# One fused Trainium2 kernel of three transformer layers: how the second layer's output rows, the router's bias logits, the last norm's gain rows and the late expert loads are arranged

## What is computed

```
for i in range(2):
    x = x + 0.5 * swiglu(rmsnorm(x), ffn1)                    # D_FF = 2816
    q, k, v, q_m = split(rmsnorm(x) @ w_in[i])
    o_m = memory_attention(q_m, k_m, v_m)                     # 4 heads
    if i == 0: o_s = chunked_rel_attention(q, k, v, bias)     # 12 heads
    else:
        o = diff_attention(q, k, v, lam)                      # 6 heads of width 128
        o_s = rmsnorm(o, b_subln) * (1 - lambda_init)
    x = x + concat(o_s, o_m) @ w_out[i]
    x = x + 0.5 * swiglu(rmsnorm(x), ffn2)
t = moba_attention(x)                                         # 8 heads
h = layer_norm(alpha * x + t, ln_g[0], ln_b[0])
logits = h @ w_router + b_router                              # 32 experts, top 4
f = sum over the 4 chosen experts of gate * expert(h)         # 1024 -> 2048 -> 1024
out = layer_norm(alpha * h + f, ln_g[1], ln_b[1])
```

## Time and profile before

| | us |
|---|---|
| runs of the kernel | 2065.43, 2066.38, 2068.64 (median 2066.38) |
| the profiled execution, its time | 2069.82 |
| its span in the profile | 2068.0 |
| PE busy in the span | 1988.8 |
| DMA queue 1 | 602.79 MB, 74.9% of 16 engines |

### The profile page before, as it was taken

How to read it: one execution, slowest core, us unless ns; L and a number is a source line. 1 busy time by engine, 2 the same in 40 slices (tenths; PEclk the granted TensorE clock), 3 DMA queues, 4 the chain that set the end, 5 groups by cost and what they waited for, 6 DMA issues and landing times.

```text
span 2068.0 us, 29157 instructions
## 1 busy us (share of the span) xinstructions
PE 1988.8 (96%) x12306; PEld 1384.8 (67%) x12306; DVE 894.7 (43%) x1070; ACT 686.3 (33%) x941; POOL 39.1 (2%) x30
## 2 busy tenths in 40 slices
PE   8999999999999998999999999999999999999997
PEld 8998768999999886999998544444343333433343
DVE  6766666676666787666645211111111111111112
ACT  5545475545555566444444111111001000101011
POOL 0700000000000000000000000000000000000000
PEclk9999999999999998999999899999999999999999
DMA  9663607556556442555296999999999999999997
GB/s 317 196 223 131 235 1 257 191 184 200 170 190 208 166 162 74 173 202 184 95 333 247 372 426 427 427 428 428 429 428 429 428 429 428 429 428 429 428 429 318
DMA packets 165568, 603.88 MB, mean 292 GB/s; under 512 B 9324, under 2 KB 102464, under 8 KB 140564
## 3 DMA queue, kind: packets, MB, share of 16 engines
q1 hardware_dynamic: 165328, 602.79, 74.9%
q10 hardware_dynamic: 164, 0.04, 0.0%
HBM read 601.71 MB, written 1.09 MB: 291 GB/s over the span
## 4 chain that ended last, share of the span: by engine, by line
PE 69%; DMA 22%; DVE 4%; ACT 3%; issue 1%; SPq 0%; DVEq 0%; ACTq 0%
PE ps L1832 13%; PE ps L1834 13%; PE ps L1833 13%; PE ps L2412 12%; DMA sb_w_free<-in_moe_w_gate_up 7%; PE ps L2436 5%; DMA sb_raw<-in_moe_w_down 5%; DMA sb_raw<-in_moe_w_gate_up 3%; DMA sb_w_free<-in_moe_w_down 3%; PE ps L2382 2%; DMA sb_nat_more<-in_moe_w_gate_up 2%; DMA sb_late_raw<-in_moe_w_down 2%; ACT sb_w_hi L669 1%; PE ps L2444 1%; PE ps L2393 1%; DVE sb_w_lo L1112 1%
## 5 line engine op out<-in xcount | busy, mean ns | idle before, releaser
L1112 DVE TENSOR_TENSOR sb_w_lo<-sb_raw,sb_w_hi 128x2048 fp32r<-128x2048 f32 x175 | 403.0, 2312 | 233.8 <-ACT sb_w_hi L669 233.3
L669 ACT ACTIVATE sb_w_hi<-sb_raw 128x2048 fp32r<-128x2048 f32 x179 | 340.5, 1912 | 167.9 <-PE ps L1834 147.6
L1832 PE MATMUL ps<-sb_xT_hi,sb_w_hi 128*128 128x256 f32 x1344 | 373.2, 278 | 0.0
L1833 PE MATMUL ps<-sb_xT_lo,sb_w_hi 128*128 128x256 f32 x1344 | 372.7, 277 | 0.0
L1834 PE MATMUL ps<-sb_xT_hi,sb_w_lo 128*128 128x256 f32 x1344 | 372.6, 277 | 0.0
L1833 PEld LDWEIGHTS ps<-sb_xT_lo,sb_w_hi 128*128 128x128 f32 x1344 | 252.8, 188 | 1.5
L1832 PEld LDWEIGHTS ps<-sb_xT_hi,sb_w_hi 128*128 128x128 f32 x1344 | 252.3, 188 | 1.7 <-DVE sb_w_lo L1112 0.2
L1834 PEld LDWEIGHTS ps<-sb_xT_hi,sb_w_lo 128*128 128x128 f32 x1344 | 253.2, 188 | 0.0
L1027 ACT ACTIVATE sb_h_rows<-ps 128x512 f32<-128x512 f32 x32 | 19.2, 599 | 424.1 <-PE ps L2412 424.1
L1707 DVE COPY sb_h_rows<-ps 128x512 f32<-128x512 f32 x31 | 21.4, 692 | 317.2 <-PE ps L2412 317.2
L1834 PE MATMUL ps<-sb_w_hi,sb_a_lo 128*128 128x512 f32 x352 | 138.5, 393 | 0.0
(11 more groups left out here) (320 smaller groups left out, 2678.8 us busy)
## 6 DMA issues: line engine op xcount, KB each, us to landing
sb_raw<-in_moe_w_gate_up SPq DMA_DIRECT2D x49, 2048.0 KB, 34.5
sb_w_free<-in_moe_w_gate_up SPq DMA_DIRECT2D x46, 2048.0 KB, 34.5
sb_w_free<-in_moe_w_down SPq DMA_DIRECT2D x24, 2048.0 KB, 33.9
sb_raw<-in_ffn_w_up SPq DMA_DIRECT2D x44, 1024.0 KB, 5.3
sb_raw<-in_ffn_w_down SPq DMA_DIRECT2D x44, 1024.0 KB, 5.0
sb_raw<-in_moe_w_down SPq DMA_DIRECT2D x22, 2048.0 KB, 33.9
sb_raw<-in_ffn_w_gate SPq DMA_DIRECT2D x43, 1024.0 KB, 5.4
sb_late_raw<-in_moe_w_gate_up SPq DMA_DIRECT2D x17, 2048.0 KB, 35.2
```

Source lines behind the costliest of these rows:

```text
L669: sc.activation(w_hi[:, c % CUT, :], raw[:, c % RAW, :], ACT.Copy).then_inc(hi_made, 1)
L1112: ve.tensor_tensor(w_lo[:, c % CUT, :], raw[:, c % RAW, :], w_hi[:, c % CUT, :].bitcast(F32), ALU.subtract).then_inc(lo_made, 1)
L1832: pe.matmul(o, l_hi, r_hi, start=start, stop=False)
L1833: pe.matmul(o, l_hi, r_lo, start=False, stop=False)
```

## The change

1. **Second layer's output rows.** ACT and DVE cut the turned rows by block (`turn_block`, pieces of 2x128 columns), block 1 as soon as it is normed. `project_blocks` does the first column half of `w_out` for block 1, turns block 0 ahead of the last two of block 1's eight tiles, then does block 0. The second column half is as before. `sub_norm` is parted into `sub_mean` and the rest; block 1's mean and root come earlier.
2. **Bias logits.** The 8 matmuls of the bias logits, the router's weights and its bias row move from the router into the end of the second layer's attention, with three matmuls that nobody reads. Around the router there are fewer of those, and block 1's first `residual` comes behind the first expert's chunks.
3. **Last norm's rows.** Three pairs of single rows (4 KB each) are loaded early. POOL splits them into three 16-bit parts, and two sets of four matmuls (`spread_last_rows`) spread the gain and the bias over the partitions: the gain goes through PSUM to SBUF by ACT, the bias stays in PSUM. The two loads of 512 KB go.
4. **Late chunks.** The last gate and up chunk and both down chunks of expert 30 come in two DMAs each with a wait for each. The scatter of expert 30 stands between the halves of expert 31's first down chunk. The kept expert is 28 in place of 29, and the loop covers steps 4 to 27. The table for the root is loaded inside `last_two`.

```diff
-KEPT_E = N_E - 3
-LOOP_S = range(5, 9)
+KEPT_E = N_E - 4
+LOOP_S = range(4, 8)
...
+                else:
+                    sp.wait_ge(trig_gains, 4)
+                    sp.dma_start(wr[:], a["moe_w_router_2"][0].rearrange("(k p) e -> p k e", p=P)).then_inc(rel_loaded, 16)
+                    sp.dma_start(lg_row[:], rows(a["moe_b_router_2"][0], N_E)).then_inc(rel_loaded, 16)
...
+                sp.dma_start(dst[:, 0:1, :], src[:, 0:1, :]).then_inc(last_gate_row, 16)
+                sp.dma_start(dst[:, 1:2, :], src[:, 1:2, :]).then_inc(slot_loaded[(t + 3) % RING], 16)
...
+                src, dst = rows_of(N_E - 2, 0), slots[(t + 4) % RING].rearrange("p (a n) -> p a n", a=4)
+                sp.dma_start(dst[:, 0:2, :], src[:, 0:2, :]).then_inc(down_rows_0, 16)
+                sp.dma_start(dst[:, 2:4, :], src[:, 2:4, :]).then_inc(slot_loaded[(t + 4) % RING], 16)
...
+            for q in (32, 64, 96):
+                sp.dma_start(narrow_rows[q:q + 1, :], a["ln_g_2"][0, 1:2]).then_inc(ln1_loaded, 16)
+                sp.dma_start(narrow_rows[q + 1:q + 2, :], a["ln_b_2"][0, 1:2]).then_inc(ln1_loaded, 16)
...
-            sp.wait_ge(chunk_used, ROUND_C * more + (MOE_C0 + KEPT_T[1] + 1))
-            sp.dma_start(ln1_gain, rows(a["ln_g_2"][0, 1], D)).then_inc(ln1_loaded, 16)
-            sp.dma_start(ln1_bias, rows(a["ln_b_2"][0, 1], D)).then_inc(ln1_loaded, 16)
...
+            step(pool.memset(ln1_parts[:], 0.0))
+            for r in range(3):
+                src, part = (t[32 * r + 32:32 * r + 34, :] for t in (narrow_rows, ln1_parts))
+                for _ in range(r):
+                    step(pool.tensor_copy(part, src))
+                    step(pool.tensor_tensor(src, src, part, ALU.subtract))
+                step(pool.tensor_copy(part, src))
...
+                sc.wait_ge(ln1_spread, 2 * r + 1)
+                sc.activation(ln1_gain, ps[:, 2:4, :].rearrange("p a b -> p (a b)"), ACT.Copy).then_inc(gain_copied, 1)
...
+            def project_blocks(g, c0, t):
+
+                pe.wait_ge(proj_read, g - 1)
+                for b in (1, 0):
+                    for kk in range(KT):
+                        c, k = c0 + kk // 4, kk % 4
+                        if (b, kk) == (1, 6):
+                            turn(nat, [(sub_normed, 2)], (0,), last=0)
+                        if k == 0:
+                            pe.wait_ge(lo_made, c + 1)
+                        turned_tile(t + 1 - b, kk)
...
+                        if kind == "diff" and n == len(groups) - 2:
+                            pe.wait_ge(prob_made, u0 + n + 1)
+                            pe.wait_ge(rel_loaded, 64)
+                            keep_busy(1, 1)
+                            router_bias(range(4))
+                        elif kind == "diff" and n == len(groups) - 1:
+                            keep_busy(1, 1)
+                            router_bias(range(4, 6))
                         values(n)
+                        if kind == "diff" and n == len(groups) - 1:
+                            keep_busy(1, 1)
+                            router_bias(range(6, 8))
...
-                    keep_busy_from_biases(3, 2)
+                    keep_busy_from_biases(1, 2)
...
+            def spread_last_rows(row, bank):
+
+                for h in range(2):
+                    for half in halves:
+                        ins = pe.matmul(ps[half, bank + h, :], ln1_sel[:, row, :], ln1_parts[:, 512 * h:512 * (h + 1)],
+                                        start=True, stop=True)
+                return ins
...
+                down_rows(t + 6, 0, laps, r, own=last_own, bank=0, first_half=ahead_rows, between=scatter_here)
                 down_rows(t + 7, 1, laps, r, True, last_own, 0)
+                spread_last_rows(1, 1).then_inc(ln1_spread, 1)
                 scatter(last=e + 2)
```

More of the change, by code:

```diff
@@ L584, in _ @@
                     step_loads(4 * it + s, s, 3 * it)
-            step_loads(N_E - 3, N_E - 3)
+            for e in range(N_E - 4, N_E - 2):
+                step_loads(e, e)
             last_loads()
@@ L796, in tile_copies, with turn_block @@
                     ins.then_inc(tiles_copied, 1)
+            def turn_block(t, b, part):
+                for q in part:
+                    sc.wait_ge(turned, 4 * t + q + 1)
+                    src = ps[:, q, :].rearrange("p (k b t) -> p k b t", k=2, b=TB)[:, :, b]
+                    sc.activation(xT_hi[:, 2 * q:2 * q + 2, b * P:(b + 1) * P], src, ACT.Copy).then_inc(turn_hi, 1)
             def sub_root(b):
@@ L1081, in first_round @@
                         step(4 * it, s, 3 * it)
-                step(0, N_E - 3, 0)
+                for s in range(N_E - 4, N_E - 2):
+                    step(0, s, 0)
                 last_two(0)
@@ L1395, in remainder @@
                     for n in range(len(groups) + 1):
+                        if n == 7 and groups[-1]["diff"]:
+                            sub_mean(1)
                         if 1 < n < len(groups):
@@ L1803, in first_round @@
                         step(4 * it, 4 * it, s, 3 * it, 0)
-                step(0, 0, N_E - 3, 0, 0)
+                for s in range(N_E - 4, N_E - 2):
+                    step(0, 0, s, 0, 0)
                 last_two(0)
@@ L2205, in remainder, with router_bias @@
                         first_block()
+                def router_bias(ks):
+                    for k in ks:
+                        ins = pe.matmul(ps[:, 0, 0:N_E], gcol[:, 70 + k:71 + k].to_broadcast([P, P]), wr[:, k, :], start=k == 0,
+                                        stop=k == KT - 1)
+                    if ks[-1] == KT - 1:
+                        ins.then_inc(bias_logits, 1)
                 def moba_ahead():
@@ L2427, in down_rows @@
                 for k in range(4):
-                    if in_halves and k == 2:
+                    if between and k == 2:
+                        between()
+                    if first_half is not None and k == 2:
                         pe.wait_ge(slot_loaded[t % RING], loaded_no(t, laps, r))
```

153 lines of the change are left out of this document (101 added, 52 removed).

## The result

The changed kernel took 2054.49 us (median of four runs, 2053.82 to 2055.03) beside 2065.90 of the kernel before (four runs, 2064.81 to 2068.64): a ratio of 0.9939, 95% interval 0.9925 to 0.9953, or 11.4 us less. The forecast was 2055.1.

The account below looks back on a forecast made before the run. The weight stream was taken to run unpaused from the first free ring slot, which bounds the end. Gains of 5.0 + 3.9 + 2.4 = 11.3 us take the median from 2066.4 to 2055.1, range 2051.0 to 2061.0.

Parts of the forecast that it names:

- Term 1: Second layer's output rows: scaling and product start earlier by block; gain 5.0 us, range 3.4 to 7.1.
- Term 2: Router: bias logits, unread matmuls and a residual leave the path; net gain 3.9 us, range 2.5 to 4.8.
- cap: Ahead of the weight stream: DMA's idle stretch of some 4 us limits what a router gain can bring.
- the upper case: Second layer's output rows: PE stays at 2.4 GHz, product's first half ends at 817.1, gain 7.1 us.
- The lower case: Second layer's output rows: clock falls as before, product's first half ends at 820.9, gain 3.4 us.
- Term 3: Tail: PE gets ahead of the last landings, table load leaves the path; gain 2.4 us, range 1.5 to 3.2.
- The sign "the last chunk's matmuls should wait for landings": End of the experts: matmuls wait for landings, last output activation some 2.4 us earlier relative to the first slot.
- A: As rival: clock stays at 2.4 GHz through the second layer's end, falls later in router; 15.1 us, 2051.3; chance 0.12.
- B: As rival: less unread work brings more half speed, into the first expert chunk or two; 5.4 us, 2061.0; chance 0.12.
- C: As rival: half speed holds through the first expert, stream loses 2.9 us a chunk; 2072.5 us; chance 0.05.
- D: As rival: PE falls behind at the end or late landing stays; gain 7.9 us, 2058.5; chance 0.08.
- E: As rival: inserted matmuls delay attention's last groups, output rows save nothing; gain 6.3 us, 2060.1; chance 0.08.

Follow-up runs that it names:

- e3: Kernel before with only the tail changes: split and spread last-norm rows, halved late chunks, expert 28 kept, table load earlier; 2064.17 us, ratio 0.9979.
- e2: Kernel before with only the bias logits and loads moved into attention, three unread matmuls there, fewer around the router, block 1's first residual later; 2062.77 us.
- e1: Kernel before with only the second layer's output rows by block; old router and tail, no added unread matmuls; 2059.24 us, ratio 0.9961.
- e10: Changed kernel with the last gate and up chunk and expert 30's two down chunks whole, one DMA and wait each; 2055.26 us.
- e7: Changed kernel with expert 29 kept rather than 28, loop steps adjusted, all else as changed; 2056.84 us.
- e6: Changed kernel without its tail changes: last-norm rows by two 512 KB loads, late chunks whole, expert 29 kept, table load where it was; 2055.06 us.
- e5: Changed kernel run again unaltered, on a second chip, beside the kernel before; 2053.95 us, ratio 0.9943.
- e4: Changed kernel without the three unread 512-column matmuls among the second layer's last attention groups, bias logits staying there; 2056.36 us, ratio 0.9945.
- e11: Changed kernel with the six 4 KB last-norm row loads issued by the scalar engine instead of the sync engine's queue; 2053.37 us.
- e8: Kernel before with only three unread 512-column matmuls added among the second layer's last attention groups; 2064.87 us beside 2064.78, ratio 1.0002.
- e9: Changed kernel with eight more unread matmuls between the router and the first expert's gather, delaying the first ring slot; 2056.23 us.

## Why the prediction held, step by step

**The sum: right, and in part by luck.** Without the router's fall, the traces give 6.3 + 2.3 + 2.5 = 11.1 us for the three terms, where 5.0 + 3.9 + 2.4 was forecast and the medians gave 11.4. Term 1 was 1.3 too small and term 2 was 1.6 too large, for reasons that have nothing to do with each other.

**What bounds the kernel: right.** The end followed the first free slot: C moved by 13.35 us, the last landing by 12.9. The evidence given for it, the idle stretch of some 4 us in the queue, was that of an execution with the router's fall; e3 has none (share 1.00 or more), and its landing follows the slot all the same. As a cap it was wrong too: in the profiled pair the router gained 8.0 us, and e2 shows all of its gain at the landing.

**Term 1, 5.0 forecast: its starts were right, its size was 1.3 too small.** The product was to start near 806.5 and did at 806.41, and x was to be updated near 820 and was at 820.04, the latter by luck: PE was done with the half at about 818.5, and DVE came 1.5 us later because of the chunk that it was cutting, a cut that the prediction took to be hidden. PE didn't wait for it. A moved by 5.3 and not by the 6.3 below; 0.9 of this was lost behind 1013 at a granted clock of 1.00, where the changed kernel's trace has the slower pace. But the 5.0 was a middle between a clock that falls (3.4) and one that doesn't (7.1). (The middle of 3.4 and 7.1 is 5.25.) It didn't, and the local stretch gained 6.3 (31.1 to 24.8): the upper case, mis-sized by 0.8. Most of this is the product: its matmuls were priced at 0.215 us, as spaced in the experts, and are 0.229 apart (811.97 to 818.15 in 27 steps), so that 48 take 11.0 us and not 10.3. The lower case was mis-sized more: with a fall (e1) the gain is 5.1, not 3.4, where the product starts 4.4 us behind the start of the fall rather than 10.1, and the fall lasts 6.8 us rather than 13.6. The charge of 1 us for inserted matmuls that don't fit at half speed was too high too: the last group's copy comes 3.00 us behind the one ahead of it with them (e10) and 2.63 without (e1), both with a fall of 6.8 us. At full clock it is 2.39 with them (804.80 after 802.41).

**Term 2, 3.9 forecast: too large for most executions, too small for the profiled one; the step behind it failed.** I took the fall from 1136.5 to 1150 as part of the kernel before, and let half speed go on in the changed one. The work taken out is worth 2.30 us (14.39 to 12.09, to 0.01 us the same in nine traces against three), where the same items stand in the prediction with 1.3 + 0.4 + 0.9 + 1.1 = 3.7; another 1.0 there, and 0.8 against it, were charged to the clock. The fall is worth 5.7 more, in those executions that have it (10 of 57 by a mean clock of 0.990 or 0.991, if that is their sign). The median gain of e2, 5.3, has an interval of 1.7 to 7.0 and doesn't tell the two apart. The step that failed is reading one profiled execution as the kernel: it lay 3.4 us above the median of the runs, the prediction said so, and carried the offset over to the profiled time (2058.5) instead of asking what it was. The changed kernel's profiled execution took 2054.72. That the offset is the router's fall isn't shown for the executions without a trace; the table of mean clocks fits it, and e3, 5.0 us above its median without that fall, shows that an offset can come from elsewhere. The expected half speed in the first expert didn't occur.

**Term 3, 2.4 forecast: right in the trace.** From landing to last outputs 3.8 became 1.3, and 15.3 us from the landing to the end became 13.0. PE's pass through the last chunks came as worked out: its first half chunk of expert 31's down weights starts at 2032.56, which is 2045.4 with the landing's 12.9 us added, where 2045.2 was forecast, and the last outputs at 2041.15, which is 2054.0. Counted from the first slot to the last outputs, the tail gained 2.0 in the pair (901.9 to 899.8), since the landing came 0.4 later behind the slot. The sign "the last chunk's matmuls should wait for landings" hardly showed: one wait of 0.58 us, at the half chunk, and 5.55 us for the last 24 records against 5.37 in e7, where nothing waited. The main step, that keeping expert 28 puts PE ahead of the landings, is shown by e7 (3.5, and 902.2 from the slot). The halves bring 0.7 (e10), the lower part of "1 to 2 us at three places, given back only in part". The table load was not tried alone. By the medians the tail is worth less, 1.1 (e6 against e5), not told apart from 2.3 by their spread, and 3.9 in e3, whose interval holds 2.3 too.

**Rivals.** A was right that the clock stays at 2.4 GHz through the second layer's end, in seven traces of eight; it let it fall later in the router, and it didn't fall there. That its 15.1 us is near the profiled pair's 15.2 is chance: its terms were 7.1, 4.8 and 3.2, and the pair has 5.3 at A, 8.0 in the router, 0.4 lost on the stream and 2.3 from the last landing to the end. I gave it 0.12, too little for what it said of 802. B and C fell: no trace of any kernel shows half speed in the first expert. Half speed does come among the early experts, though, for 3.4 us in e4, 6.8 in e10 and 6.8 in e11, between 1264 and 1277, each beginning near a product of 32 rows (`sb_narrow_rows`), with PE busy all the while. In e10:

```profile
1272.00:1276.00 4.00, 4.00 (x18) 0.50 1.03 438
```

There it cost nothing that shows: from the first slot to the last landing these three take 898.2 to 898.4 us.

D fell in the form given: PE waited 0.58 us at a half chunk and still gained the tail. E fell: the stretch gained 6.3 us with the inserted matmuls in place. The stream kept its 4.89 us a chunk with the halves in it, since D - C did not change by more than it scatters (898.5 against 898.1 in the pair, 898.3 in e10, 897.6 to 899.6 in all).

## What to carry to other kernels

Read one profiled execution against the spread of the runs before pricing a half-speed stretch: if it lies some us above the median, ask which stretch of it others don't have. A chain of short matmuls and waits ahead of dense work is worth shortening twice, for its own time and because the half speed ended sooner where dense work began sooner: at 808.4 with the product from 805.99 (e1), at 815.7 with it from 812.12 (before). Behind a long stream, the lead of the engine that consumes it is set by where its cached pieces lie: moving the kept piece one period earlier gained more here (2.2 us, e7) than cutting the last transfers (0.7 us, e10). And when parts of a sum can be off in either direction, check them one by one: here two of three were off by more than 1 us and the total by 0.1.

## What the runs showed of the hardware

The granted clock falls in some executions of the same code and not in others. In the router's old form, 13.7 us at 0.50 appeared in one of four traces, and the same instructions cost 20.10 or 14.39 us. Near 802 the fall began at 801.6 (e1) to 803.1 (e8), in e3 at 806.3, and lasted 6.8 to 13.7 us. At a granted clock of 1.00 matmuls of 256 columns came every 113.6 ns or every 117.8 ns, the latter in e3 from 540 to 680, and what sets the pace is open. A fall among the experts (6.8 us in e10 and e11) left the time from the first slot to the last landing at 898.3 and 898.4 us. Some 2 us behind the issue of the first slot's DMA the transfer rate dipped with the engines still counted as full, 324 GB/s at a share of 1.22 in e11 and 344 at 1.26 in e6, with or without the six small loads. And a transfer queue without idle time did not mean that the stream had stopped depending on the first free slot (e9).
